# Expert stage: outputs stored per group of four units and per column block, expert weights in rows of 8192 bytes

## The reference, cut to what matters

```python
def expert_block(args):
    xb, e = args
    hu = xb @ w13[e]                       # (tokens, 1024) @ (1024, 1024)
    a_, b_ = jnp.split(hu, 2, axis=-1)
    return (jax.nn.silu(a_) * b_) @ w2[e]  # (tokens, 512) @ (512, 1024)
...
out = jax.ops.segment_sum(ys * row_w[:, None], row_tok, num_segments=T)
```

## Time and profile before

| what | value |
|---|---|
| median of 3 runs | 2355.97 us (2354.79 to 2361.44) |
| profiled execution, span from first to last instruction | 2356.3 us; no time around it is recorded for this execution |
| expert stage, first weight copy to last `y_out` | 568.4 to 1182.4 us |
| PE busy over the span | 2145.3 us (91%) |
| DMA over the span | 370.12 MB, mean 157 GB/s |
| units computed (outputs stored) | 80, that is 20 groups |

### The profile page before, as it was taken

One profiled execution on the slowest core, in us unless ns is written; L12 is line 12 of the kernel. 1 busy time (PEld: TensorE's weight loads), 2 busy tenths in 40 slices (PEclk: granted clock), 3 DMA queues, 4 the chain that ended last, 5 costly groups with the idle time before them and its releaser, 6 DMA issues. The chain is left out here.

```text
span 2356.3 us, 43499 instructions
## 1 busy us (share of the span) xinstructions
PE 2145.3 (91%) x15936; PEld 1602.9 (68%) x15936; DVE 1237.3 (53%) x1539; ACT 823.3 (35%) x1198; POOL 564.1 (24%) x379
## 2 busy tenths in 40 slices
PE   5999988995787997878779989899999999999998
PEld 4788766783444554434458867688888888888887
DVE  7888356425676886757746458534332123212244
ACT  5122165113566885756622038512100001000023
POOL 1433211310000000000025632123323323233243
PEclk9999999996898998988869999999999999999999
DMA  7633042329999699999752300111111111111113
GB/s 276 245 126 118 28 161 66 134 90 409 410 360 333 242 380 353 355 356 354 293 194 90 95 26 1 34 47 45 45 53 45 47 51 45 54 45 52 47 56 123
DMA packets 104883, 370.12 MB, mean 157 GB/s; under 512 B 7948, under 2 KB 19052, under 8 KB 104428
## 3 DMA queue, kind: packets, MB, share of 16 engines
q1 hardware_dynamic: 86476, 326.68, 38.7%
q10 hardware_dynamic: 13008, 23.07, 2.6%
q0 software_dynamic: 5328, 19.40, 2.2%
HBM read 337.61 MB, written 31.51 MB: 157 GB/s over the span
## 5 line engine op out<-in xcount | busy, mean ns | idle before, releaser
L1673 PE MATMUL moe_hu<-x_res,moe_xt 128*32 128x256 f32 x5120 | 338.0, 407 | 63.6 <-DVE moe_xt L1592 24.1
L1570 DVE COPY x_res<-moew_raw 128x2048 f32 x243 | 270.4, 1135 | 171.4 <-DMA moew_raw<-in_w 106.0
L1673 PEld LDWEIGHTS moe_hu<-x_res,moe_xt 128*32 128x32 f32 x5120 | 162.5, 115 | 194.9 <-issue 58.7
L244 PE MATMUL ff_acc<-ff_yh,ff_w_hi 128*128 128x512 f32 x704 | 274.4, 390 | 0.0
L244 PE MATMUL ff_acc<-ff_yl,ff_w_hi 128*128 128x512 f32 x704 | 273.9, 389 | 0.0
L244 PE MATMUL ff_acc<-ff_yh,ff_w_lo 128*128 128x512 f32 x704 | 273.9, 389 | 0.0
L1570 ACT ACTIVATE x_res<-moew_raw 128x2048 f32 (+1 forms) x121 | 197.7, 1634 | 97.8 <-DMA moew_raw<-in_w 69.6
L212 POOL CAST ff_w_hi<-ff_w_raw 128x1024 fp32r<-128x1024 f32 (+1 forms) x82 | 81.9, 998 | 547.1 <-PE ff_acc L244 547.1
L244 PE MATMUL ff_acc<-xh,ff_w_hi 128*128 128x512 f32 x480 | 188.2, 392 | 3.3 <-DVE ff_w_lo L228 2.6
L214 POOL TENSOR_TENSOR ff_w_lo<-ff_w_raw,ff_w_hi 128x1024 fp32r<-128x1024 f32 (+1 forms) x82 | 188.6, 2300 | 6.6
L244 PE MATMUL ff_acc<-xl,ff_w_hi 128*128 128x512 f32 x480 | 187.3, 390 | 0.0
(11 more groups left out here) (426 smaller groups left out, 3734.4 us busy)
## 6 DMA issues: line engine op xcount, KB each, us to landing
moew_raw<-in_w SPq DMA_DIRECT2D x192, 1024.0 KB
ff_w_raw<-in_w_up SPq DMA_DIRECT2D x44, 512.0 KB, 3.5
mid_w_raw<-in_w_qkv SPq DMA_DIRECT2D x24, 512.0 KB
in_w_raw<-in_w_in SPq DMA_DIRECT2D x23, 512.0 KB, 3.6
xbc<-in_w_ada SPq DMA_DIRECT2D x20, 512.0 KB, 7.9
y_scratch<-acc_sq ACTq DMA_DIRECT2D x80, 128.0 KB
ff_w_raw<-in_w_down SPq DMA_DIRECT2D x16, 512.0 KB, 3.6
x_res<-in_w_ada SPq DMA_DIRECT2D x14, 512.0 KB, 4.1
```

The costliest lines, as they stand in the source:

```text
L244: m = pe.matmul(o, w[:, b, k * P:(k + 1) * P], x[:, k, h:h + HALF], start=(k == 0 and t == 0), stop=(k == kt - 1 and t == 2))
L1570: m = e.activation(to, src, ACT.Copy) if k == "act" else e.tensor_copy(to, src)
L1673: m = e.matmul(hu[u % 2][rows(j), 0:2 * FW].rearrange("p (a f) -> p a f", a=2), xt[:, t, rows(u)], w[:, :, FW * j:FW * (j + 1)], start=(t ...
```

## The change

Two things are changed.

1. The outputs are stored per group and column block. `ysb` is now a buffer of its own with room for two groups (`[P, 2, CT, YW]`), and `xt` takes the place in `acc_sq`. `send(g, j)` stores the column block j of all four units of group g at once: 32 partitions (tokens) by 4 units by 256 elements, still 128 KB and rows of 1024 bytes. In slots 1, 2 and 3 of the next group ACT issues the blocks (0), (1, 2) and (3), in slot 0 none; the last group's four go out one behind the other at the end. The target's outermost dimension is now the 32 tokens. `send` first waits for the block's store of the group before. `y_out` of a group's first unit waits for all four stores of two groups before; `y_out` and `send` each have a no-operation ahead, and the buffer is chosen by the group's number modulo 2 in a register.
2. The host lays out `w13` and `w2` so that a partition's two rows of a pair lie one behind the other (`pairs`): the load of a pair is 128 rows of 8192 bytes, in place of 256 of 4096 bytes. The bytes and the number of loads stay.

```diff
-                        e.dma_start(self.raw[:, n, :].rearrange("p (a d) -> p a d", a=2), self.expert_pair(o, p)).then_inc(self.s_w[p], 16)
+                        e.dma_start(self.raw[:, n, :], self.expert_pair(o, p)).then_inc(self.s_w[p], 16)
...
     def expert_pair(self, x, p):
-        src, at = (self.ins["w13"], 2 * P * p) if p < KT // 2 else (self.ins["w2"], 2 * P * (p - KT // 2))
-        rows = src[x, at:at + 2 * P, :] if isinstance(x, int) else src[bass.ds(x, 1), at:at + 2 * P, :].rearrange("o r d -> (o r) d")
-        return rows.rearrange("(a p) d -> p a d", p=P)
+        src, n = (self.ins["w13"], p) if p < KT // 2 else (self.ins["w2"], p - KT // 2)
+        return src[x, n] if isinstance(x, int) else src[bass.ds(x, 1), n].rearrange("o p d -> (o p) d")
...
-            xt = st.sb("xt", [P, KT, P])
+            xt = self.acc_sq[:, :].rearrange("p (k t) -> p k t", k=KT)
-            ysb = self.acc_sq[:, :].rearrange("p (u c) -> p u c", u=CT)
+            ysb = st.sb("ysb", [P, 2, CT, YW])
...
-                        e.dma_start(dst.rearrange("p (a d) -> p a d", a=2), self.expert_pair(source, p)).then_inc(s_w[p], 16)
+                        e.dma_start(dst, self.expert_pair(source, p)).then_inc(s_w[p], 16)
...
-                    for b in range(CT):
-                        e.sem_inc(s_sent[b], 16)
+                    for j in range(CT):
+                        e.sem_inc(s_sent[j], 32)
...
-                    def send(v, u):
-                        e.wait_ge(s_yout, v + 3)
-                        e.dma_start(self.y_dram[bass.ds(TOK * v, TOK), :].rearrange("t (j c) -> j t c", j=CT), ysb[:, u, :]).then_inc(s_sent[u], 16)
+                    def send(g, j):
+                        e.wait_ge(s_yout, CT * g + (CT + 2))
+                        e.wait_ge(s_sent[j], 16 * g + 32)
+                        e.nop(nofuse=True)
+                        src = ysb[rows(j), bass.ds(g % 2, 1), :, :].rearrange("t o u c -> t (o u) c")
+                        dst = self.y_dram[bass.ds(P * g, P), YW * j:YW * (j + 1)].rearrange("(u t) c -> t u c", u=CT)
+                        e.dma_start(dst, src).then_inc(s_sent[j], 16)
...
-                            if u >= 2 or not first:
-                                send(unit(u - 2), (u - 2) % CT)
+                            if not first:
+                                for j in ((), (0,), (1, 2), (3,))[u]:
+                                    send(g - 1, j)
...
-                    send(CT * n + (CT - 2), CT - 2)
-                    send(CT * n + (CT - 1), CT - 1)
-                    for b in range(CT):
-                        e.wait_ge(s_sent[b], 16 * n + 32)
+                    for j in range(CT):
+                        send(n, j)
+                    for j in range(CT):
+                        e.wait_ge(s_sent[j], 16 * n + 48)
...
-                    def y_out(v, u, sent):
+                    def y_out(v, u, g):
                         e.wait_ge(s_downfree, FF // P * v + 2 * (FF // P))
-                        e.wait_ge(s_sent[u], 16 * sent)
-                        e.tensor_copy(ysb[:, u, :], yp[u % 2][:, 0:YW]).then_inc(s_yout, 1)
+                        if u == 0:
+                            for j in range(CT):
+                                e.wait_ge(s_sent[j], 16 * g + 16)
+                        e.nop(nofuse=True)
+                        b = g % 2 if isinstance(g, int) else bass.ds(g % 2, 1)
+                        to = ysb[:, b, u, :] if isinstance(g, int) else ysb[:, b, u, :].rearrange("p o c -> p (o c)")
+                        e.tensor_copy(to, yp[u % 2][:, 0:YW]).then_inc(s_yout, 1)
...
+def pairs(w):
+
+    E, K, N = w.shape
+    return np.ascontiguousarray(w.reshape(E, K // (2 * P), 2, P, N).transpose(0, 1, 3, 2, 4)).reshape(E, K // (2 * P), P, 2 * N)
...
-        "w13": np.ascontiguousarray(a["w13"][0]), "w2": np.ascontiguousarray(a["w2"][0]),
+        "w13": pairs(a["w13"][0]), "w2": pairs(a["w2"][0]),
```

More of the change, by code:

```diff
@@ L1552, in experts @@
             s_silu, s_act, s_aturn, s_at, s_yout = (st.sem(n) for n in ("silu", "act", "aturn", "at", "yout"))
-            s_sent = [st.sem(f"sent{b}") for b in range(CT)]
+            s_sent = [st.sem(f"sent{j}") for j in range(CT)]
             s_xturn = st.sem("xturn")
@@ L1782, in group @@
                             if u >= 2 or not first:
-                                y_out(unit(u - 2), (u - 2) % CT, g + 1 if u >= 2 else g)
+                                y_out(unit(u - 2), (u - 2) % CT, g if u >= 2 else g - 1)
                             def more():
@@ L1800, in _ @@
                     copy_down(e, "dve", CT * n + (CT - 1), expert(e, CT * n + (CT - 1)))
-                    y_out(CT * n + (CT - 2), CT - 2, n + 1)
-                    y_out(CT * n + (CT - 1), CT - 1, n + 1)
+                    y_out(CT * n + (CT - 2), CT - 2, n)
+                    y_out(CT * n + (CT - 1), CT - 1, n)
     def middle(self):
```

## The result

| | before | changed |
|---|---|---|
| median of 4 runs | 2356.74 us (2354.79 to 2361.44) | 2278.13 us (2276.0 to 2282.33) |
| ratio | 1 | 0.9661, 95% interval 0.9642 to 0.968 |
| profiled span | 2356.3 us | 2276.6 us |
| last `y_out` ends | 1182.4 us | 1108.6 us |

A forecast was written before the change was run, and what follows sets the result against it. Outside 760 to 860 us (PE-bound), weight DMA was taken as the bound, held back by four engines carrying the stores. Terms -2 - 15 - 45 - 6 + 2 = -66 us from 2356.3 gave 2290 us, range 2270 to 2316.

The forecast's parts named there:

- The four engines as the cause: Expert stage: stores load only four of 16 DMA engines, and weight loads wait for those four.
- Per expert: DMA time per expert on the slowest engine: 17.15 us instead of 20.2, a ratio of 0.85.
- 660 to 760 us: Expert-stage stretch where the DMA rate has dropped: a gain of 15 us.
- PE's stretch: 760 to 860 us, where the weight ring is full and PE sets the pace: no gain.
- 860 us to the end: Late DMA-bound stretch: 45 us gained, plus 6 us from entering it with the ring refilled further ahead.
- Rows of 8192 bytes: Weight loads: eight fewer packets per engine save 0.06 us a load, 0.35 us per expert; bounds nothing to twice that.
- the first rival: Spreading the stores does nothing and only the longer weight rows act: 10 us gained, 2346 us; chance 6%.
- ACT's issues: Two store issues in slot 2 delay the silu in slot 3 within PE's stretch: +2 us, +4 at most.
- The end: Last group's four store issues instead of two, against a faster landing: 0, between -2 and +3 us.
- the spreading does nothing: Rival: rate falls for another reason or new stores use few engines too; 2346 us, chance 6%.
- slower by `y_out`: Rival: spread stores land late and DVE waits before `y_out` in every group; 2384 us, chance 4%.
- DMA all but ceases to be the bound: Rival: long rows save twice as much and the lead is kept, 16.8 us per expert; 2274 us, chance 8%.

The follow-up runs named there:

- o_flat: Kernel before with only the store's target rewritten as 128 rows of 256 elements in memory order, 16 engines per store, rows permuted within a unit: 2284.84 us, ratio 0.9694.
- g_unit16: Kernel before with each unit's store issued as four DMAs of one column block, 32 tokens outermost, 16 engines, no grouping: 2287.55 us, ratio 0.9685.
- a_stores: Changed kernel with the old weight layout, so grouped stores on 16 engines and 4096-byte weight rows: 2285.32 us, ratio 0.9692.
- b_rows: Kernel before with only the new 8192-byte weight rows, stores still on four engines: 2371.33 us, ratio 1.0063.
- h_early4k: Changed kernel with the first 17 weight loads read from an extra copy in the old layout, in 4096-byte packets: 2276.71 us, ratio 0.9643.
- d_route4k: Changed kernel with the first 17 weight loads meant to be cut to 4096 bytes; void, packets stayed at 8192: 2276.11 us, ratio 0.9657.
- m_rows2k: Kernel before with weight pairs laid out in four pieces, rows of 2048 bytes, stores still on four engines: 2377.61 us, ratio 1.007.

## Why the prediction was right

- **The four engines as the cause** was right. The small packets (4 then, 16 now), o_flat and g_unit16 show it, and the rate is 422 GB/s. The step from four engines to the same four each time was not spelled out in the prediction; the runs bear it out as said above.
- **Per expert** 17.15 us were forecast and 16.5 measured (six loads with what goes beside them). The sum was oversized at two places. The loads: 8 x 311 + 9 ns are 2.50 us, six are 15.0 where I had 15.35; in a_stores, the same kernel with 4096-byte rows, a load packet has a mean of 162 ns and a load 2.60 us, so the long rows save 0.10 us a load and not 0.06. And the overlap: with 0.86 us of gathers and 0.96 of stores the measured packets make 16.8 us, but their times add up to 102% of the window, so some overlap, which gives 16.5. The kernel before has the same fault: my sum had 20.2 us; the 20.0 beside it came from counting issues, and by bytes, as the 16.5 are counted, it is 19.6. The difference between the two kernels, which makes the gain, was forecast as 3.05 us and is 3.1.
- **660 to 760 us:** 15 us forecast, 17.5 measured (units 8 to 20). **PE's stretch:** 0 and 0. **860 us to the end,** with the lead: 45 + 6 forecast, 55.9 measured from unit 32 on. The last 17 us stayed.
- **Rows of 8192 bytes:** 311 ns a packet against 46 + 7 x 36 to 39 = 298 to 319 ns; the price of the packet was inside its bounds. That the gain holds beside any store was wrong, though the step stood only in the first rival: there, rows alone were 2346 us, and b_rows gave 2371. The forecast itself had 16 engines, where it holds.
- **ACT's issues:** +2 us forecast, 0 measured. I took 1.05 us an issue from the old store; the new one takes 0.33. In the changed kernel's stretch at PE's pace the two issues of slot 2 take 0.93 us together and silu follows without idle time:

```profile
789.36 1.09 PE L1655 MATMUL moe_xturn<-consts,moew_xg 128*128 128x128 f32 x8
...
807.40 0.93 ACTq L1725 DMA_DIRECT2D y_scratch<-moe_ysb  x2
808.44 0.28 ACT L1713 ACTIVATE moe_act<-moe_hu 128x128 f32<-128x128 f32 x1
...
813.47 1.09 PE L1655 MATMUL moe_xturn<-consts,moew_xg 128*128 128x128 f32 x8
```

A group takes 24.11 us as before (24.12).

- **`y_out`:** no wait for stores; they land in 2.0 to 7.9 us. **The end:** 1.4 us less, within -2 to +3.
- **Not foreseen:** the late start behind the `h_scratch` stores, 7 us, which cost nothing that the runs tell from noise (h_early4k's last output is 3 us earlier). The other 4.7 us of the late start were there before the first of these stores was issued (532.3 against 527.6 us) and do not go with the rows: a_stores with the old ones has 531.9, d_route4k with the new ones 527.6.
- **The rivals:** "the spreading does nothing" and "slower by `y_out`" fell with the packet counts and the landings; what the second describes did happen in b_rows, by way of the issue. The 358 GB/s of the Trainium skill (DMA: Bandwidth & Descriptors, Where 436 GB/s comes from) is not the limit here: 422 GB/s over 230 us. "DMA all but ceases to be the bound" was put at 2274 us, and 2278 lies nearer to it than to the forecast's 2290. Part of its condition did come about: the long rows save 0.10 us a load, between the forecast's 0.06 and the 0.12 of that case, and an expert takes 16.5 us against its 16.8. But the weights' DMA is still the bound from 860 us on (share 1.02, and 56 us of waits in the stage), as the forecast had it.
- The 4.5 us in untouched stages are no part of the mechanism but luck; without them the time would be near 2282 us.

## What to carry to other kernels

Look at a DMA's outermost dimension on both sides: the store with 4 there used four of the 16 engines, and the loads that need all 16 then ran at the pace of those four, 357 GB/s in place of 412. The busy share did not show it (0.98); the GB/s in a busy stretch and the small packets per transfer did. Before lengthening the rows of a bulk load, look at what shares its engines: each of the other queue's packets can wait for one of yours. And price a DMA's issue with the pattern that it will have: here it differed by a factor of three, 1.05 against 0.34 us.

## What the runs showed of the hardware

- The issue of the same 128 KB store takes 1.05 us on ACTq for four engines and 0.34 us for sixteen (o_flat). For the 32 KB stores it is 0.32 us on sixteen, 0.68 on eight and 0.63 on four, so of these three it is fewer than sixteen that costs, not how few.
- An issue can hold the issuing engine's queue when its earlier DMAs have fallen behind: up to 7.6 us in b_rows, where a store spans 9.8 us, with the compute instructions behind it; in the kernel before (6.4 us) and m_rows2k (4.05 us) no issue took over 1.2 us. How many may be outstanding was not measured.
- Engines of unequal load still show a busy share of 0.97 to 0.98. Load packets of 4096 bytes have a mean of 184 ns there (680 to 760 us, by the packet records) at a median of 159, with a tail up to 1.5 us; in o_flat from 860 to 1060 us the longest took 178 ns. So part of an engine's wait appears to be recorded as time of a packet, which would keep the busy share up; that is a reading of these numbers and was not tested.
- Packets take 46 ns for 1024 bytes, 84 for 2048, 159 for 4096 and 310 for 8192 (medians; the 1024 are stores, the others loads): some 8 ns and 38 ns per KB. With all engines busy that gave 411 GB/s at 4096 and 422 at 8192.
